# A PEER layer's gate multiply moves from VectorE to GpSimd, between the row gathers

## The reference

```
g = jax.nn.softmax(vals, axis=-1).astype(xb.dtype)
a = jax.nn.gelu(jnp.einsum('nd,nhkd->nhk', xb, u_tab[e]))
return jnp.einsum('nhk,nhkd->nd', g * a, v_tab[e])
```

## Time and profile before

| | us |
|---|---|
| time, median of 3 runs (2382.51 to 2389.28) | 2382.54 |
| time of the profiled execution | 2390.65 |
| its span from the first to the last instruction | 2388.9 |
| PE / DVE / ACT / POOL busy | 2212.1 / 1818.9 / 1257.2 / 431.1 |

### The profile page before, as it was taken

One profiled execution on the slowest core, in us unless ns is written; L12 is line 12 of the kernel. 1 busy time (PEld: TensorE's weight loads), 2 busy tenths in 40 slices (PEclk: granted clock), 3 DMA queues, 4 the chain that ended last, 5 costly groups with the idle time before them and its releaser, 6 DMA issues. The chain is left out here.

```text
span 2388.9 us, 33531 instructions
## 1 busy us (share of the span) xinstructions
PE 2212.1 (93%) x11984; PEld 1201.8 (50%) x11984; DVE 1818.9 (76%) x3809; ACT 1257.2 (53%) x1695; POOL 431.1 (18%) x395
## 2 busy tenths in 40 slices
PE   6799898798689798999999999989999999999997
PEld 3476666444356566444555554544444444444443
DVE  1566643545576775788999999973799999999999
ACT  1465572324566772553444445766655566555653
POOL 0011110000011020022323232430122222222220
PEclk9799999899799899999999999999999999999999
DMA  9555572000366584467899999897778777887771
GB/s 383 230 193 187 176 230 95 9 27 9 143 236 203 210 292 171 162 230 247 270 350 305 348 306 349 310 356 281 287 290 310 288 295 292 308 300 291 292 285 71
DMA packets 192074, 574.29 MB, mean 240 GB/s; under 512 B 18464, under 2 KB 52032, under 8 KB 184256
## 3 DMA queue, kind: packets, MB, share of 16 engines
q1 hardware_dynamic: 113872, 329.69, 40.2%
q0 software_dynamic: 47104, 167.80, 19.0%
q10 hardware_dynamic: 30960, 75.07, 8.1%
HBM read 455.48 MB, written 117.00 MB: 240 GB/s over the span
## 5 line engine op out<-in xcount | busy, mean ns | idle before, releaser
L297 PE MATMUL u_ps<-h_hi,lin_hi 128*128 128x512 f16 x1024 | 389.7, 381 | 5.3 <-PEq L74 5.3
L297 PE MATMUL u_ps<-h_lo,lin_hi 128*128 128x512 f16 x1024 | 389.7, 381 | 0.0
L297 PE MATMUL u_ps<-h_hi,lin_lo 128*128 128x512 f16 x1024 | 389.5, 380 | 0.0
L279 DVE SCALAR_TENSOR_TENSOR lin_lo<-lin_raw,lin_wsc,lin_hi 128x1024 f16<-128x1024 f32 x132 | 169.4, 1284 | 161.4 <-ACT lin_hi L273 161.0
L1888 POOL DMA_INDIRECT row<-v_dram,picked x128 | 179.1, 1400 | 577.5 <-DVE acc L2523 449.3
L1953 POOL DMA_INDIRECT row<-u_rows_dram,picked x128 | 175.9, 1374 | 518.1 <-DVE dot_junk L2137 354.1
L273 ACT ACTIVATE lin_hi<-lin_raw,lin_wsc 128x1024 f16<-128x1024 f32 x132 | 151.1, 1146 | 194.9 <-DVE lin_wsc L138 146.0
L2394 PE MATMUL ps_w<-oh_turned,oh_buf 128*128 128x128 f16 x1024 | 224.3, 219 | 4.0 <-ACT region L2066 3.7
L2634 PE MATMUL y_ps<-region 128*128 128x512 f16 x512 | 194.7, 380 | 1.4 <-PEq L1892 1.4
L2636 PE MATMUL y_ps<-region 128*128 128x512 f16 x512 | 194.8, 380 | 0.0
L2635 PE MATMUL y_ps<-region 128*128 128x512 f16 x512 | 194.6, 380 | 0.0
(11 more groups left out here) (397 smaller groups left out, 4474.7 us busy)
## 6 DMA issues: line engine op xcount, KB each, us to landing
lin_raw<-w_all_dram SPq DMA_DIRECT2D x132, 512.0 KB
act_scratch<-activated ACTq DMA_DIRECT2D x128, 256.0 KB
wgt_scratch<-region ACTq DMA_DIRECT2D x64, 512.0 KB
region<-v_dram SPq DMA_DIRECT2D x15, 2048.0 KB, 7.5
oh_buf<-v_dram SPq DMA_DIRECT2D x15, 2048.0 KB
proj<-w_mod_dram SPq DMA_DIRECT2D x16, 1536.0 KB, 12.0
act_buf<-w_all_dram SPq DMA_DIRECT2D x38, 512.0 KB, 7.6
lin_hi<-split_scratch SPq DMA_DIRECT2D x64, 256.0 KB
```

The lines of the kernel that those rows point to most:

```text
L279: nc.vector.scalar_tensor_tensor(out=self.lo[b][:], in0=self.raw[b][:], scalar=self.wsc[:, self.col(b)], in1=self.hi[b][:], op0=ALU.mult, ...
L297: last = nc.tensor.matmul(self.ps[b % 2][:, half, 0:ts.stop - ts.start], w_[:, kc, :], x_[:, kc, ts], start=(j == 0 and kc == 0), stop=(j ...
```

## The change

`multiply` takes the engine as an argument. In the last stage, `mixed` no longer calls it, and the GpSimd stream calls it instead. The multiplies of groups 0 and 1, in the stage before, stay on DVE. The four multiplies of group g + 2 stand in GpSimd's stream in front of the last two gathers that belong to group g (`end` is the number of rows added when group g is done).

```
-            def multiply(self, dve, i, gp, c_):
+            def multiply(self, eng, i, gp, c_, unit=nc.vector):
                 if c_ == 0:
-                    dve.wait_ge(s(f"vp_ld_w{gp}"), 16 * i + 16)
-                    dve.wait_ge(s(f"vp_ld_a{gp}"), 16 * i + 16)
+                    eng.wait_ge(s(f"vp_ld_w{gp}"), 16 * i + 16)
+                    eng.wait_ge(s(f"vp_ld_a{gp}"), 16 * i + 16)
                 col = self.g_act[gp][:, c_, :].rearrange("p (b n) -> p b n", n=WB)
-                nc.vector.tensor_tensor(col, col, self.w_raw[gp][:, :, c_ * WB:c_ * WB + WB], ALU.mult
-                                        ).then_inc(s(f"vp_mult{gp}"), 1)
+                unit.tensor_tensor(col, col, self.w_raw[gp][:, :, c_ * WB:c_ * WB + WB], ALU.mult
+                                   ).then_inc(s(f"vp_mult{gp}"), 1)
...
             @block.gpsimd
             def _(pool):
-                for j in range(NG, PICKS):
-                    pool.wait_ge(s("row_add"), j - NG + 1)
-                    second_row(j)
+                def rows_to(end):
+
+                    nonlocal row_next
+                    while row_next < min(end, PICKS):
+                        pool.wait_ge(s("row_add"), row_next - NG + 1)
+                        second_row(row_next)
+                        row_next = row_next + 1
+                row_next = NG
+                for g in range(VGROUPS):
+                    end = upto[min(g + 1, VGROUPS - 1)]
+                    rows_to(end + NG - 2)
+                    if g + 2 < VGROUPS:
+                        for c_ in range(VG):
+                            second.multiply(pool, (g + 2) // 2, g % 2, c_, nc.gpsimd)
+                    rows_to(end + NG)
...
                     rows = rows_of(2 * i + gp)
-                    for c_ in range(VG):
-                        second.multiply(dve, j, ngp, c_)
                     add_up(i, gp, 0)
```

## The result

The changed kernel takes **2437.64 us** (median of 4 runs, 2434.55 to 2443.7), the kernel before 2382.53 us in the same comparison. The ratio is 1.0249, with a 95% interval of 1.0227 to 1.027: 55 us slower. The forecast was 2436.

What follows compares the result with a forecast made beforehand. Prediction: neither PE nor DVE has room, and the ring is as tight as PE. 30 x 1.74 = 52 us plus 1.28 for the ISA instruction, together +53.5, on the 2382.5 us median gives 2436; range 2400 to 2510.

Steps and rivals of the forecast that it cites:

- the ring: Loop from second row add through multiplies, ACT, PE's total and splits to next second row add, 21.24 us per group.
- PE's floor: Time PE alone needs per group in the last stage: 21.05 us, with the kernel before 0.38 us above it.
- One multiply, 1.2 us: One of the four multiplies on GpSimd, 512 elements per partition: 1.2 us, with bounds of 0.53 and 1.39.
- The ring's first part, 7.85 us: From second row add's end to last multiply's end: 1.30 + 0.55 + 1.2 + 4 x 1.2 = 7.85 us, before 6.11.
- the rival in which nothing excludes: GpSimd's multiplies and DVE read SBUF side by side: no change, 2383 to 2390 us; chance 0.08.
- +1.74 us and +52: Growth at PE's total: 1.74 us more per group, 30 times, 52 us.
- the five-row groups: Four of the 30 groups, where the gather waits for the third row add: 2 us more, left inside the range.
- The third collision: Rival: next group's first row add goes before the last multiply; +100 us, about 2482, or 2493 at 1.39; chance 0.22.
- The ISA instruction, 1.3 us: Instruction before GpSimd's first multiply, which may load code: 1.28 us taken from ACT's table load, lower bound nothing.
- DVE's room: DVE loses four multiplies, 2.40 us per group, so it has 2.4 us of room and is no longer a bound.
- The late gathers: A group's last two gathers wait about 6 us for the multiplies; rows needed over 10 us later, costed at nothing.

Runs made afterwards that it cites:

- 5.13 us (2374): Also called the best kernel: changed kernel with the gather behind the multiplies and the context rows' running sum in PSUM from row 17 on; 2374.35 us, ratio 0.9972.
- 6.24 (2395): Changed kernel with row adds reading one input from PSUM instead of the row buffer from row 17 on, context sum left out; 2395.01 us, ratio 1.0056.
- 7.08 (2410): Changed kernel with one gather moved from ahead of GpSimd's multiplies to behind them; 2410.24 us, ratio 1.0119.
- The fillers on PE: Changed kernel with six matmuls, whose result nobody reads, put ahead of PE's total from group 4 on; 2445.2 us, ratio 1.0276.

## Why the prediction was right

**What bounds.** Right for the ring. The five measured lengths of its first part put the kernels in their order: 5.13 us (2374), 6.11 (before, 2383), 6.24 (2395), 7.08 (2410), 7.73 (2438). The time follows its length as long as it is the longer one. In size it does so for the typical group alone: 0.13 us more would be 4 us at 2395, and 12 were measured, for the reason given there. PE's floor was off: I took 21.05 us per group, with a step of 0.60 us at the total, which still held a wait. Free of it the step is 2007.38 - 2007.03 = 0.35 us, and from total to total it is 20.86 us. So by this floor up to 29 x (21.43 - 20.86) = 17 us were to be had, and not 11; the best kernel took 6 of them.

**One multiply, 1.2 us.** Measured 1.25. The estimate of 1.12 us, from the figure in the Trainium skill's "GPSIMD Engine Reference", section "Performance versus the Vector engine", was 10% short at this size.

**The ring's first part, 7.85 us.** Measured 7.73: 0.36 + 0.94 as stated, then 5.0 us of multiplies where 4.8 was said, and 1.43 of waiting where 1.75 was. The waits are those named, for the third and the fourth row add. That the waits also go the other way was an inference from GpSimd's gathers alone; it is now shown by row adds of 1.63 and 2.32 us and by the run with the rows from PSUM, which also answers the rival in which nothing excludes. "SBUF — State Buffer" in the Trainium skill, section "Who interferes with whom", says as well that a DVE instruction with at most one SBUF input, outside the 2-port modes, doesn't contend with GpSimd, and here this is the cure: the set fell from 6.43 to 4.93 us.

**Per group and in sum, +1.74 us and +52.** The typical group grew by 1.56, 45 us over 29; the long groups gave another 13. The term that was mis-sized is the one for groups that are not typical. I had put the five-row groups at 2 us and left them inside the range; the three of them between the first and the last set gave 1.6, but the third collisions (6.4 us) and the lower clock (3 to 4) stood in no sum. So the nearness of 2436 to 2437.64 is in part luck: 7 us too much for the typical groups and 1.2 for the ISA instruction stand against 13 that were not counted, and the parts ahead of the stage moved as well.

**The third collision** was a rival with 0.22, for all groups. It came in 5 of 30, at about 1 us each in the set (7.4 against 6.43). I said that PE's lateness holds the block adds back; that is what happens in most of the others, but by little: in the timeline above the last multiply started at about 2012.26 - 1.25 = 2011.01, and the row add stands at 2011.03. The fillers on PE tipped ten of 30 over; with the reordered row adds it was four.

**The ISA instruction, 1.3 us.** It cost 2 x 32 ns. The gather ahead of it ended at 1699.44, and the first multiply stands at 1699.55. The Trainium skill's "GPSIMD Engine Reference" gives about 6 us for a first call (section "Instruction dispatch"); the trace here, with its 0.1 us, doesn't agree, unless that time was spent earlier, where it doesn't show.

**DVE's room** was there and of no use: DVE waits 32.4 us for PE's blocks, and its free time lies there. **The late gathers** were nearly hidden: DVE waited 7.8 us in all for rows, in three waits of 3.4 us or less, all behind groups with five rows, and behind each of them DVE still had to wait for PE's total, 0.26 to 1.58 us.

What stays open is why the 6.33 us row add (below) did not get in between two multiplies, and what tips a group over into the third collision.

## What to carry to other kernels

Work that is moved from VectorE to GpSimd is not beside VectorE's if both read SBUF through two-input instructions: count each neighbour with two SBUF inputs as a wait, in both directions, before counting the engine's free time. One operand in PSUM on VectorE's side took the conflict away at the same duration (a row add took 1281 ns in the mean with the sum in PSUM, 1279 in the kernel before), so look for an accumulator that can live there. And an engine's busy share says little on what the move is worth: find the ring with its longest link, and place the moved work where that link begins.

## What the hardware showed that I had not expected

A row add on DVE can be held much longer than by one multiply. In the group at 2332 us the four multiplies ran through, and the row add, recorded from 2332.71 on, stood behind all of them (DVE, then GpSimd):

```profile
2332.71 6.33 DVE L2535 SCALAR_TENSOR_TENSOR acc<-row,picked,acc 128x1024 f32<-128x1024 f32 x1
...
2332.07 0.94 POOL L1888 DMA_INDIRECT row<-v_dram,picked  x1 [12.65 <-issue]
2333.03 4.92 POOL L464 TENSOR_TENSOR eq_buf<-eq_buf,sc_buf 128x512 f32<-128x512 f32 x4
```

It ended at 2339.04, 1.09 us after the set's end at 2337.95. In the timeline of the typical group the row add at 2007.05 got its turn after one multiply. It isn't a single accident: the kernel with the fillers has one of 6.32 us and the one with the reordered row adds one of 6.37, each beside four multiplies that ran through.

The issue of an indirect gather, which reads only a column of indices, is held by two-input DVE instructions too: 1.93 us in place of 0.94 beside row adds back to back, in the changed order as in the kernel before. But not always. This one of the kernel before starts beside the multiplies of the earlier trace rows, 1.20 us behind the start of the first and right behind another gather, and is not held at all; three more like it are at the same place of their sets:

```profile
2037.79 0.94 POOL L1888 DMA_INDIRECT row<-v_dram,picked  x1 [0.30 <-issue]
```

Nothing here shows why.

When PE had waited 2.67 us at its total, its clock came back at 1.2 GHz in place of 2.4, for steps of 0.43 us instead of 0.215 over some 6 us. That cost only 3 to 4 us in all. PE makes up for it: its next wait for ACT, at the total of 1991.72, was only 0.30 us, where it is 1.51 in the group after that.
